# Recurrence gates computed as three terms of weight and input halves, two gates of a head in one matmul, two heads beside each other

## The reference

```
c = centred_depthwise_conv(u_x, conv_w, conv_b)            # 512 channels = 8 heads of 64
r = sigmoid(block_diag(c, wa, ba));  i = sigmoid(block_diag(c, wx, bx))
log_a = -8 * r * softplus(-lam);     a = exp(log_a)
h[t] = a[t] * h[t-1] + sqrt(1 - a*a) * i * c               # once forward, once backward
y_c = (h_forward + h_backward) * gelu(u_gate)
```

## Time and profile before

| | |
|---|---|
| median of 3 runs | 1112.31 us (1110.53 to 1113.14) |
| profiled execution | 1111.36 us, span from first to last instruction 1109.1 us |
| granted TensorE clock, mean | 0.996 |
| TensorE matmul busy | 1085.8 us |
| VectorE / ScalarE busy | 851.0 / 708.3 us |
| gate matmuls (L1718) busy, all four blocks | 14.7 us |

### The profile page before, as it was taken

The page is one execution under the profiler, slowest core; times in us unless marked ns, Lnnn a source line. Parts: engine busy times, 40 slices in busy tenths (PEclk is TensorE's granted clock), DMA queues, the critical chain, the costliest instruction groups (busy, mean ns, idle before and its releaser), DMA issues.

```text
span 1109.1 us, 18916 instructions
## 1 busy us (share of the span) xinstructions
PE 1085.8 (98%) x6751; PEld 960.2 (87%) x6751; DVE 851.0 (77%) x1034; ACT 708.3 (64%) x932; POOL 46.6 (4%) x41
## 2 busy tenths in 40 slices
PE   7999999999999999999999999999999999999995
PEld 6989989989999998998989987788888888888883
DVE  6976885875544556587696777999999999999996
ACT  6467764454444445446866446788888888888883
POOL 1300000000000000200000000000000000000010
PEclk9999999999999999999999999999999999999998
DMA  9955446565556657845445549999999999999971
GB/s 296 253 171 168 125 143 193 169 207 184 178 156 224 189 188 198 240 153 177 132 130 181 166 139 398 396 394 396 396 394 401 391 393 381 393 372 398 383 277 40
DMA packets 140971, 281.71 MB, mean 254 GB/s; under 512 B 26800, under 2 KB 27120, under 8 KB 140912
## 3 DMA queue, kind: packets, MB, share of 16 engines
q1 hardware_dynamic: 136688, 266.69, 70.5%
q0 software_dynamic: 3776, 13.64, 3.4%
q10 hardware_dynamic: 448, 0.59, 0.2%
HBM read 275.11 MB, written 5.77 MB: 253 GB/s over the span
## 4 chain that ended last, share of the span: by engine, by line
PE 85%; DVE 8%; ACT 4%; issue 2%; DMA 0%; DVEq 0%; ACTq 0%
PE ps L1541 26%; PE ps L1543 26%; PE ps L1542 26%; DVE w_lo L943 2%; PE ps L1718 1%; ACT w_hi L544 1%; DVE yl L943 1%; PE ps L1943 1%; PE ps L1636 1%; PE ps L1746 1%; PE ps L1692 1%; ACT p_t L725 1%; PE ps L1857 1%; PE ps L1757 1%; DVE small L1165 1%
## 5 line engine op out<-in xcount | busy, mean ns | idle before, releaser
L943 DVE TENSOR_TENSOR w_lo<-raw,w_hi 128x1024 fp32r<-128x1024 f32 x268 | 323.3, 1224 | 153.1 <-ACT w_hi L544 151.1
L544 ACT ACTIVATE w_hi<-raw 128x1024 fp32r<-128x1024 f32 x268 | 280.5, 1059 | 172.5 <-PE ps L1543 169.2
L1541 PE MATMUL ps<-xh,w_hi 128*128 128x256 f32 x960 | 274.5, 286 | 0.0
L1542 PE MATMUL ps<-xl,w_hi 128*128 128x256 f32 x960 | 271.6, 283 | 0.0
L1543 PE MATMUL ps<-xh,w_lo 128*128 128x256 f32 x960 | 271.6, 283 | 0.0
L1541 PEld LDWEIGHTS ps<-xh,w_hi 128*128 128x128 f32 x960 | 184.1, 192 | 2.6 <-issue 2.1
L1542 PEld LDWEIGHTS ps<-xl,w_hi 128*128 128x128 f32 x960 | 184.1, 192 | 0.4
L1543 PEld LDWEIGHTS ps<-xh,w_lo 128*128 128x128 f32 x960 | 184.0, 192 | 0.0
L1541 PE MATMUL ps<-w_hi,xh 128*128 128x512 f32 x432 | 170.5, 395 | 0.5 <-DVE xl L1351 0.3
L1542 PE MATMUL ps<-w_lo,xh 128*128 128x512 f32 x432 | 168.4, 390 | 0.0
L1543 PE MATMUL ps<-w_hi,xl 128*128 128x512 f32 x432 | 168.4, 390 | 0.0
(11 more groups left out here) (248 smaller groups left out, 1511.8 us busy)
## 6 DMA issues: line engine op xcount, KB each, us to landing
mix<-in_moe_w_gu_dram SPq DMA_DIRECT2D x112, 512.0 KB, 8.6
raw<-in_w_in_dram SPq DMA_DIRECT2D x96, 512.0 KB, 4.3
raw<-in_moe_w_gu_dram SPq DMA_DIRECT2D x80, 512.0 KB, 8.3
mix<-in_moe_w_down_dram SPq DMA_DIRECT2D x80, 512.0 KB, 8.7
raw<-in_ffn_w_gu_dram SPq DMA_DIRECT2D x48, 512.0 KB, 4.0
raw<-in_w_branch_dram SPq DMA_DIRECT2D x24, 512.0 KB, 3.7
raw<-in_ffn_w_down_dram SPq DMA_DIRECT2D x24, 512.0 KB, 4.6
raw<-in_w_out_dram SPq DMA_DIRECT2D x16, 512.0 KB, 3.6
```

The source lines that it names most:

```text
L544: act.activation(halves(u)[0], src, ACT.Copy).then_inc(hi_done, 1)
L943: dve.tensor_tensor(w_l, place(u)[0], w_h.bitcast(F32), ALU.subtract).then_inc(lo_done, 1)
L1541: mm(dst, ah, bh, start=first, stop=False, skip_group_check=True)
L1542: mm(dst, ah, bl, start=False, stop=False, skip_group_check=True)
```

## The change

The convolution output and the recurrence weights are split into halves like the other operands, and the gates are computed in three terms. The weights of the two gates of a head lie side by side, so that one matmul has 64 rows and 128 columns and gives gate a of the head on PSUM partitions 0 to 63 and gate x on 64 to 127. The two heads of a channel block use the upper and the lower half of the array's rows and write two different banks. Since gate and head no longer lie as the channels do, ScalarE's tanh reads one half of the partitions at a time and writes it to the half where the channels are: eight instructions of 64x256 a gate.

```diff
-        wlru = sb("wlru", [P, 2, 2, BC, HD])
+        wlru = sb("wlru", [P, 2, BC, 2, HD])
+        wlru_hl = [f[:, 2 * D:3 * D].rearrange("p (d m o) -> p d m o", d=2, m=BC) for f in (yhf, ylf)]
+        conv_hl = [f[:, 0:D].rearrange("p (m s) -> p m s", m=BC) for f in (yhf, ylf)]
+        def lru_out(m, hh):
+            return 4 + 2 * (m // 2) + hh, SEQ * (m % 2)
...
@@ scalar, mixer
+                    if k == AT_CONV + 2:
+                        act.wait_ge(wlru_in, 16 * 8 * (l + 1))
+                        act.activation(yhf[:, 2 * D:3 * D], wlru[:, :, :, :, :].rearrange("p d m g o -> p (d m g o)"),
+                                       ACT.Copy).then_inc(wlru_h, 1)
+                    if k == AT_CONV + 5:
+                        act.wait_ge(conv_ok, l + 1)
+                        act.activation(yhf[:, 0:D], cflat, ACT.Copy).then_inc(conv_h, 1)
...
-                                i = act.activation(lru[:, g, SEQ * m:SEQ * m + SEQ],
-                                                   ps[:, 4 + 2 * g + m // 2, SEQ * (m % 2):SEQ * (m % 2) + SEQ],
-                                                   ACT.Tanh, scale=0.5, bias=col2[:, o:o + 1])
+                                for hh in range(2):
+                                    bank, c0 = lru_out(m, hh)
+                                    q = slice(HD * hh, HD * hh + HD)
+                                    i = act.activation(lru[q, g, SEQ * m:SEQ * m + SEQ],
+                                                       ps[HD * g:HD * g + HD, bank, c0:c0 + SEQ],
+                                                       ACT.Tanh, scale=0.5, bias=col2[q, o:o + 1])
...
@@ vector, mixer (ahead of the Fourier work of the same k)
+                    if k == AT_CONV + 2:
+                        dve.wait_ge(wlru_h, l + 1)
+                        dve.tensor_tensor(ylf[:, 2 * D:3 * D], wlru[:, :, :, :, :].rearrange("p d m g o -> p (d m g o)"),
+                                          yhf[:, 2 * D:3 * D].bitcast(F32), ALU.subtract).then_inc(wlru_l, 1)
+                    if k == AT_CONV + 5:
+                        dve.wait_ge(conv_h, l + 1)
+                        dve.tensor_tensor(ylf[:, 0:D], cflat, yhf[:, 0:D].bitcast(F32), ALU.subtract).then_inc(conv_l, 1)
...
@@ tensor, mixer
                                 pe.wait_ge(yb_l, l + 1)
-                                pe.wait_ge(conv_ok, l + 1)
-                                pe.wait_ge(wlru_in, 16 * 8 * (l + 1))
-                            for g in range(2):
-                                for m in range(BC):
+                                pe.wait_ge(wlru_l, l + 1)
+                                pe.wait_ge(conv_l, l + 1)
+                            for m in range(BC):
+                                for n, (w, x) in enumerate(((0, 0), (0, 1), (1, 0))):
                                     for hh in range(2):
+                                        bank, c0 = lru_out(m, hh)
                                         q = slice(HD * hh, HD * hh + HD)
-                                        ins = mm(ps[q, 4 + 2 * g + m // 2, SEQ * (m % 2):SEQ * (m % 2) + SEQ],
-                                                 wlru[q, d, g, m, :], conv_t[q, m, :], start=True, stop=True)
+                                        ins = mm(ps[:, bank, c0:c0 + SEQ], wlru_hl[w][q, d, m, :],
+                                                 conv_hl[x][q, m, :], start=(n == 0 and m % 2 == 0), stop=(n == 2),
+                                                 skip_group_check=True)
                             ins.then_inc(lru_ps, 1)
```

More of the change, by code:

```diff
@@ L256, in build @@
         f1_ps, ut_a, ut_d, f2_ps, yb_full, yb_h, yb_l = sem("f1_ps"), sem("ut_a"), sem("ut_d"), sem("f2_ps"), sem("yb_full"), sem("yb_h"), sem("yb_l")
+        wlru_h, wlru_l, conv_h, conv_l = sem("wlru_h"), sem("wlru_l"), sem("conv_h"), sem("conv_l")
         conv_ok, lru_ps, lru_tanh, lru_dec, mult_in, mult_ok, scanned = (
@@ L368, in load_tables @@
                     for d in range(2):
-                        sp.dma_start(wlru[hh * HD:(hh + 1) * HD, d, g, :, :],
+                        sp.dma_start(wlru[hh * HD:(hh + 1) * HD, d, :, g, :],
                                      w[l, d, hh::2, :, :].rearrange("m c o -> c m o")).then_inc(wlru_in, 16)
```

## The result

The changed kernel is slower: 1124.32 us median (1122.25 to 1127.97, 6 runs) against 1112.63 us (1110.53 to 1114.54, 6 runs) of the kernel before beside it, ratio 1.0111, 95% interval 1.0088 to 1.0134. The direction was forecast, the size was not: 1115.6 us was predicted with 1119.0 as the upper end. The profiled execution took 1123.38 us with a span of 1121.2 us, 12.0 us more than that of before (span 1109.1).

A forecast was written before the change was run, and what follows sets the result against it. TensorE bounds the kernel, but loses what the VectorE/ScalarE chain is late at L1178: 2.4 + 0.9 = +3.3 us, its 7.4 us gain spent waiting. 1111.36 + 3.3 = 1114.7, plus 0.95 gives 1115.6 us; range 1110.5 to 1119.

The forecast's parts named there:

- The bound and the chain: First scores to low half of attention (L1178): VectorE and ScalarE form a chain; its delay arrives whole at TensorE, +3.3 us.
- The formula 4A - 8.1: Two layers' shift at L1178 in us, A being what the two tanh groups of a direction add; zero at A = 2.0.
- The tanh step: ScalarE's gates: eight half tanh at the full ones' 0.36 us step, +1.44 us a gate, +11.5 us in all.
- the first scores: Start of attention: they wait for the last tanh, at 103.5 us, but that wait is not last.
- the upper bound: ScalarE's gate tanh: each half costs its whole 0.490 us with no overlap, +2.5 us a gate.
- (b): Gate tanh: a half-height one costs half, earlier gates pull the chain forward, 5.2 us less, 1107.1 us; chance 0.13.
- TensorE's block: Gate matmuls: twelve pairs side by side, 1.75 us a block against 3.60, gaining 7.4 us over four blocks.
- Rival (a): Gate block no shorter than 24 matmuls in a row, 3.2 us; 2.6 us more, 1118.2 us; chance 0.14.
- The splits: Before the forward gates: two added splits a layer on ScalarE and VectorE delay L1147 by 2.28 us.
- Rival (c): Around table loads and square roots: uncounted slack absorbs 0.5 to 1 us a layer; 1113.5 us; chance 0.25.
- waits of TensorE: Before layer 0's forward gates, before first scores and at L1178: together some 10 us; under 7 us would refute.
- The warning on the reading of PSUM: Gates: packing speeds up TensorE but not PSUM reading; TensorE loses 7.4 us of work, ScalarE gets 11.5 us.

The follow-up runs named there:

- the runs of four: Changed kernel with ScalarE's tanh halves reordered, four of one head half then four of the other: 1119.13 us, ratio 1.0057.
- the full tanh: Changed kernel with four full-height tanh a gate, leaving out the alignment, so gates and channels do not match: 1106.02 us, ratio 0.9941.
- the old gate blocks: Kernel before, only tanh altered: four extra full tanh a gate into an unused place, 1117.24 us; or each tanh cut into two halves, 1125.11 us.
- the four runs with more work on ScalarE: Changed kernel 1124.32 us, it with tanh halves reordered 1119.13; kernel before with four extra full tanh a gate 1117.24, with tanh halves 1125.11.
- the runs of four with attention at 30: Changed kernel with tanh halves reordered in fours and attention two units later, from k = 30 instead of 28: 1116.02 us, ratio 1.0034.

## Why the prediction was right or wrong

- **The bound and the chain: right.** Slower because ScalarE and VectorE, not TensorE, set the stretch from the backward tanh to L1178. The formula 4A - 8.1 gives 11.3, 5.5 and -5.2 us (its floor) for the changed kernel, the runs of four and the full tanh; the stretches show 12.6, 6.3 and -5.4 us. With the old gate blocks 5.0 and 12.8 us were worked out, and the stretches show 5.3 and 13.6.
- **The tanh step: wrong, and nearly the whole miss.** The term "eight instructions at a step of 0.36 us, +1.44 us a gate" was mis-sized: it measured 0.48 us and +2.4 us. It enters the sum four times for each 1 us of A: (4.85 - 2.88) x 4 = 7.9 us, from 3.3 to 11.3. That leaves under 1 us: 1111.36 + 11.3 + 0.95 = 1123.6 against 1124.3 us. With the larger term one statement on the path failed too. The prediction said of the first scores that their wait for the last tanh is not the last to end; it ended last in both layers, and TensorE stood for 4.0 us. The text did name the upper bound, no overlap, +2.5 us a gate; put through the same formula (A = 5.0) it gives 11.9 us and 1124.2 us, the measured time. The mistake that made the range too narrow was not to carry that bound into it. It also never became a rival with a chance, while the lower bound, +0, did, as (b).
- **TensorE's block: right.** 1.62 us against 1.75 worked out. Rival (a), no overlap of the two heads, fell. The Trainium skill (TensorE: Matmul & The Clock Gate, LDWEIGHTS) gives a load P/1.2 ns, 107 ns for 128 columns, so two in a row would be 0.21 us, an estimate. The trace shows no such bound: the two loads of a pair start together, and pairs follow 0.12 us apart.
- **The splits: right.** 2.0 + 0.35 us worked out, 2.0 + 0.5 measured with nothing else changed; the gates of layer 0 start behind a wait of 1.30 us, at 65.78 us against 65.9 worked out.
- **Rival (b): fell in its premise, right in its sum.** A half tanh does not cost half (0.469 against 0.490 us). With the added cost taken away, its 5.2 us came.
- **Rival (c), about the same: fell.** There was no hidden slack: in the four runs with more work on ScalarE the stretches grew by 0.2 to 0.7 us a layer more than the formula says. Where this remainder comes from was not found.
- **Said of the profile after:** waits of TensorE of some 10 us, measured 16.0; the first L1187 (before: L1163) at about 108.6 us, measured 112.84, later by the four longer tanh groups ahead of it. The fall of the clock was not foreseen, and matmuls in it count as busy longer (0.41 against 0.28 us each): TensorE's busy time fell by 1.9 us, not 7. In the runs of four with attention at 30, which has the same matmuls and no such fall, it is 1079.3 us, 6.5 less than before.
- **The warning on the reading of PSUM** (the Trainium skill, TensorEngine Tiling (Array Packing), PSUM Bottleneck): the section says that tiling speeds up TensorE but not the evacuation of PSUM, which may become the bottleneck. The runs agree with it in the direction only. Packed gates with full tanh are some 5 us faster than before, with tanh halves 12 us slower, so it was not the packing that made the reading the bottleneck, but the layout of its result, which doubled the number of reading instructions.

## What to carry to other kernels

Price an instruction that is cut in two by its step in the new company, not by the step of its whole: the overlap of neighbours may be what made it cheap. Where a bound of an unseen form is written down, push it through the same sum as the chosen value and let the range reach there. Work taken off the engine that is busy 98% of the time is worth, in a stretch where the others arrive last, only what it lets them start earlier: 7.8 us here with the tanh unchanged. Ask there which of them gets work added. When a median moves by less than the spread of one kernel, compare executions with the same granted clock.

## What the runs showed of the hardware

Consecutive ScalarE tanh instructions of 256 columns with PSUM as source started 0.36 us apart when they wrote the same partitions, be it all 128 or the same 64, and 0.47 to 0.49 us apart when one wrote partitions 0 to 63 and the next 64 to 127. A half takes 0.45 to 0.48 us and a full one 0.47 to 0.52 (up to 0.59 at the end of eight full ones in a row), so what the change of partitions takes away is the overlap. Whether a result moves to the other half of the partitions makes no difference. It is enough that the destination and the bias column change: in the changed kernel and in the runs of four the source keeps its partitions throughout a gate. Destination and bias column were not separated, and a change of the source alone was not tried.

Two matmuls of 64 rows and 128 columns on the two halves of the array's rows, each with its weight load, ran beside each other: their starts lie 3 ns apart in the changed kernel, and pairs follow every 0.12 us, as single full-size matmuls of 256 columns do.
